# Rotary embedding of the first attention layer: the sine product on VectorE moved behind a pair's score evictions

## The chip, the cores and the metric

The kernel runs on one core of one Trainium2 chip. The metric is device time in microseconds (us) of one execution; lower is better. Before the change it is 1165.88 us, the median of three runs (1165.79 to 1166.37).

## The reference, cut to what matters

Two transformer blocks of two layers each run on a sequence of 256 tokens with model width 1024, in float32. The change touches only the first layer of the first block, whose attention starts like this:

```
z = h @ a_w_in[i]
q = z[..., :w].reshape(B, S, N_DIFF_HEADS, 2, HEAD_DIM)
k = z[..., w:2 * w].reshape(B, S, N_DIFF_HEADS, 2, HEAD_DIM)
...
q = _apply_rope(q, cos, sin)      # [x1*c - x2*s, x2*c + x1*s] over the two halves of each head
k = _apply_rope(k, cos, sin)
...
o_self = _diff_attention(q, k, v, lam, lam_init, a_subln[i])
o_mem = _memory_attention(qm, mem, a_mem_norm[i], a_w_mem_kv[i])
```

So each query and key value is multiplied by a cosine, its partner from the other half of the head by a sine (with a sign), and the two products are added. Only then can the scores of these heads be computed.

## The kernel before, in words

Each engine has its own program, written out in order; engines wait for one another by semaphores. All values are kept transposed: features on the 128 partitions, the 256 tokens along the row. Weights are streamed from HBM in units of 128x1024 into a ring of four slots (`raw`); ScalarE (ACT) rounds a unit to `w_hi` (L1185) and VectorE (DVE) computes the rest `w_lo` (L1651, called a split below). TensorE (PE) multiplies with both.

The stage `in_a` makes query and key tiles of the first layer and runs the attention between them. The function `fused` gives every engine the same frame: step `s` is tile `2s`, then `between(s - 1)`, then tile `2s + 1`, then `behind(s - 1)`. On VectorE these are:

- a tile: `evict` (L1670, PSUM bank times the norm's scale into `Z`, counted by `tile_out`), then the split of a weight unit three tiles ahead;
- `between(p)`: `rotated(j)` for `j = s - 2`, then `normalised` for the two score units of pair `p - 1` (L1979 to L1990: the softmax weights, counted by `p_ready`), then small pieces of later attention steps (L2015, L2022);
- `behind(p)`: `masked` for the two units of pair `p` (L1967: the scores leave their banks, called score evictions here), then L2039 in later steps.

Pair `j` of the six rotary pairs is the query and key tile `2 + 2j` and `3 + 2j` of `Z`. Its rotation has three parts. SyncE (SP), whose program issues weight loads and these transfers in one queue, waits until tile `3 + 2j` has been evicted and then issues four DMAs of 64 KB that exchange the halves of each head into `ROT` (L520, counted by `rot_in`). GpSimd (POOL) multiplies `Z` by the cosine (L2224) at the same time. VectorE multiplies `ROT` by the sine (L2030) as soon as `rot_in` is complete, and adds the two (L2034, counted by `roped`). In the text below, these two are the sine product and the sum.

On TensorE a step is the 24 matmuls of tile `2s`, the output products of an earlier pair, the 24 matmuls of tile `2s + 1`, the scores of pair `p` (L959), and the transposes of the softmax weights of pair `p - 1` (L976), which wait for `p_ready`. TensorE takes all of it in this order. Tiles use two PSUM banks in turn, so tile `t + 2` starts only when tile `t` has been evicted.

The second layer (`in_b`) uses the same functions with another lag; its order stays as it is.

Of the kernel before, what the change touches and what calls it, by code (L numbers as in the profile page):

```python
# [98 lines left out]
FUSED = {"in_a": ("mem_a", "diff"), "in_b": ("mem_b", "moba"), "in_sb": ("stick",), "in_fox": ("forget",)}  # L99
LAG = {"in_a": 1, "in_b": 0, "in_sb": 1, "in_fox": 1}  # L100
# [24 lines left out]
def build_program(nc, ins, out):  # L125
# [7 lines left out]
    with ctx:  # L133
        def sb(name, shape, dt=f32):
            return ctx.enter_context(nc.sbuf_tensor(name, shape, dt))
# [73 lines left out]
        ROT = sb("ROT", [P, 4, TOK])  # L209
# [135 lines left out]
        ROPE_PAIRS = SELF_W // P  # L345
# [82 lines left out]
        def pair_of(name):  # L428

            units = attention_units(name)  # L430

            def pair(p):
                return units[2 * p:2 * p + 2] if 0 <= p < len(units) // 2 else []
            return pair
# [5 lines left out]
        def evicted(name, p):  # L440

            pair, q = pair_of(name), p - AHEAD[name] - 1
            return [pair(at)[1] for at, late in ((q - 1, True), (q, False))
                    if pair(at) and stands_late(name, at) == late]
# [1190 lines left out]
        def _(dve):  # L1635
# [294 lines left out]
            def attention(name):  # L1930
                pair, ahead = pair_of(name), AHEAD[name]
# [7 lines left out]
                def masked(u):  # L1939

                    n, mem = u["n"], u["mem"]
                    _, whole = geometry(u)

                    forget = u["kind"] == "forget"

                    def pieces(ap):
                        return ap.rearrange("p (a c) -> p a c", c=P) if mem or forget else ap

                    def mask(qt, cols):
                        if forget:  # L1950
                            kept = forget_buf[:, n % 4, :].rearrange("p (a c) -> p a c", c=P)
                            return kept[:, 2:3, :] if qt == 0 else kept[:, 0:4:3, :]
                        return no_mask if mem else mask_in[:, cols]
                    b = bank[4 + n % 2]
                    dve.wait_ge(s_done, n + 1)
                    if n >= 4:
                        dve.wait_ge(exp_done, n - 3)
                    if stick:
                        if n - u["first"] >= 4:
                            dve.wait_ge(arg_ready, n - u["first"] - 3)  # L1960
                        nc.vector.scalar_tensor_tensor(s_buf[:, n % 4, 0:whole], b[:, 0:whole], SCALE, mask_ex[:],
                                                       ALU.mult, ALU.add).then_inc(s_out, 1)
                        return
                    if forget:
                        dve.wait_ge(f_ready, n - u["first"] + 1)
                    for qt, cols in enumerate(query_tiles(u)):
                        last = nc.vector.tensor_tensor_reduce(  # L1967
                            out=pieces(s_buf[:, n % 4, cols]), in0=pieces(b[:, cols]),
                            in1=mask(qt, cols), scale=-SCALE, scalar=3.0e38, op0=ALU.add, op1=ALU.min,
                            accum_out=unit_bias[:, n % 4, qt:qt + 1])  # L1970
                    last.then_inc(s_out, 1)
# [50 lines left out]
                    nc.vector.scalar_tensor_tensor(H[:, j, :], H[:, j, :], subln_s[:], sub_rms[:, j % 2, :],  # L2022
                                                   ALU.mult, ALU.mult).then_inc(sub_scaled, 1)

                def rotated(j):

                    pair = ROPE_PAIRS * list(FUSED).index(name) + j
                    rot = ROT[:, 2 * (pair % 2):2 * (pair % 2) + 2, :]
                    dve.wait_ge(rot_in[pair % 2], 64 * (pair // 2 + 1))
                    nc.vector.tensor_tensor(rot, rot, rope_s[:].unsqueeze(1).broadcast_to([P, 2, TOK]),  # L2030
                                            ALU.mult).then_inc(sin_done, 1)
                    dve.wait_ge(sin_done, pair + 1)
                    dve.wait_ge(cos_done, pair + 1)
                    nc.vector.tensor_tensor(Z[:, 2 + 2 * j:4 + 2 * j, :], turned, rot, ALU.add).then_inc(roped, 1)  # L2034

                def sub_low(u):
                    j = u["j"]
                    dve.wait_ge(sub_hi, j + 1)
                    nc.vector.tensor_tensor(o_lo[:, j, :], H[:, j, :], o_hi[:, j, :].bitcast(f32),  # L2039
                                            ALU.subtract).then_inc(sub_lo, 1)  # L2040

                def between(p):

                    j = p + LAG[name] - 2
                    last_tile = 2 * (p + LAG[name]) + 1 == LAST_TILE.get(name)
                    turns = "mem_" in FUSED[name][0] and 0 <= j < ROPE_PAIRS
                    if turns and not last_tile:
                        rotated(j)
                    if stick and p == len(heads["stick"]) // 2 - 1:
                        for u in pair(p):  # L2050
                            masked(u)
                    for u in pair(p - 1):
                        log_weights(u) if stick else normalised(u)
                        if turns and last_tile and u["half"] == 0:
                            rotated(j)
                        if last_tile and u["half"] == (not stick):
                            evict(name, LAST_TILE[name])
                    for u in evicted(name, p):
                        if not u["diff"]:
                            out_lo(u)  # L2060
                    for u in evicted(name, p - 1):
                        if u["diff"]:
                            sub_scale(u)

                def behind(p):

                    for u in pair(p):
                        if not stick or p < len(heads["stick"]) // 2 - 1:
                            masked(u)
                    for u in evicted(name, p - 1):  # L2070
                        if u["diff"]:
                            sub_low(u)
                return between, behind

            nc.vector.memset(log_ms[:], 0.0).then_inc(warm_ready, 1)
# [39 lines left out]
            def lambda_difference():  # L2115
# [6 lines left out]
            values("in_a", {1: lambda: memory_lows(0), 3: memory_sums, 4: lambda: memory_lows(KT // 2)})  # L2122
            dve.wait_ge(tile_out, RING)
            fused("in_a", lambda s: query_key_tile("in_a", s), attention("in_a"), 3,
                  {(0, 0): scale_memory, (0, 1): lambda_sums, (1, 1): lambda_difference, (10, 1): lambda: split_early("out_a")})
            out_projection("out_a", "up_a")
            project("up_a", *relu("up_a"))
            project("down_a", before=residual("down_a", [("in_b", h1_hi, h1_lo), ("q_b", h2_hi, h2_lo)]))
            values("in_b")
            fused("in_b", lambda s: query_key_tile("in_b", s), attention("in_b"), 2,  # L2130
                  {(9, 0): lambda: split_early("out_b")})
            out_projection("out_b", "up_b")
# [3 lines left out]
            values("in_sb", {4: lambda: final_rows(range(0, 3)), 5: lambda: final_rows(range(3, 6)),  # L2136
                             6: lambda: final_rows(range(6, KT))})
            fused("in_sb", lambda s: query_key_tile("in_sb", s), attention("in_sb"), 3,
                  {(8, 0): lambda: split(0, RING, plan["out_sb"]["unit"] + RING - 2, KT),
                   (10, 0): lambda: split_early("out_sb"), (11, 0): lambda: split_early("out_sb", RING)})  # L2140
# [274 lines left out]
```

## Time and profile before

| | before |
|---|---|
| median of 3 runs | 1165.88 us (1165.79 to 1166.37) |
| the profiled execution | 1165.88 us, of which 1164.1 us are the span of the trace |
| busy share of the span | PE 99%, PEld 92%, DVE 76%, ACT 65%, POOL 29% |
| granted TensorE clock, mean | 0.999 of full speed |
| chain that ended last, by engine | PE 88%, DVE 5%, ACT 3%, DMA 1% |

The busy time of PE includes time in which a matmul stands in the pipeline waiting, so 99% is an upper bound of its work. The chain is followed back from the last instruction to what released each one; its shares are over the whole span, and single stages look different.

### The profile page before, as it was taken

How to read it: one execution, taken by the hardware profiler on the slowest of the kernel's cores; microseconds unless marked ns; L12 is line 12 of the kernel's file. 1: busy time of each engine (PE TensorE's matmuls, PEld its weight loads, DVE VectorE, ACT ScalarE, POOL GpSimd, SP SyncE). 2: the span in 40 equal slices, each digit the busy share in tenths (PEclk: the TensorE clock that was granted, in tenths of full speed). 3: DMA queues.
4: the chain of work that ended last, by engine and by line, in shares of the span. 5: the costliest groups of instructions: out<-in, count | busy, mean ns of one | idle time of the engine just before them, and what ended most of it. 6: DMA issues, size and time to landing. Idle time of an engine off the chain costs nothing.

```text
span 1164.1 us, 25960 instructions
## 1 busy us (share of the span) xinstructions
PE 1146.7 (99%) x8640; PEld 1068.2 (92%) x8640; DVE 882.5 (76%) x1494; ACT 753.2 (65%) x1373; POOL 337.9 (29%) x313
## 2 busy tenths in 40 slices
PE   8999999999999999999999999999999999999998
PEld 7988999999898999999899889999889988999987
DVE  7888777666579877766759978999566776898954
ACT  7766655455565755545558878888456666888842
POOL 3230355300012245522303305544000320455500
PEclk9999999999999999999999999999999999999999
DMA  8654556655645455665654346655645634565562
GB/s 316 205 147 140 178 194 202 199 189 189 221 160 162 147 194 192 203 224 181 212 186 146 128 164 195 201 198 198 217 145 186 246 132 141 188 203 200 196 217 101
DMA packets 64054, 216.62 MB, mean 186 GB/s; under 512 B 7776, under 2 KB 10992, under 8 KB 63984
## 3 DMA queue, kind: packets, MB, share of 16 engines
q1 hardware_dynamic: 63808, 215.17, 56.0%
q8 instruction: 41, 0.67, 0.2%
q10 hardware_dynamic: 176, 0.54, 0.1%
q14 instruction: 29, 0.24, 0.1%
HBM read 211.47 MB, written 1.06 MB: 183 GB/s over the span
## 4 chain that ended last, share of the span: by engine, by line
PE 88%; DVE 5%; ACT 3%; DMA 1%; issue 1%; POOL 1%; SPq 0%; DVEq 0%; ACTq 0%; POOLq 0%
PE bank L824 11%; PE bank L825 11%; PE bank L826 11%; PE bank L822 9%; PE bank L819 5%; PE bank L691 4%; PE bank L693 4%; PE bank L692 4%; PE bank L742 4%; PE bank L744 4%; PE bank L743 4%; PE bank L959 2%; PE bank L976 2%; DVE w_lo L1651 2%; PE bank L620 2%; PE bank L621 1%
## 5 line engine op out<-in xcount | busy, mean ns | idle before, releaser
L1651 DVE TENSOR_TENSOR w_lo<-raw,w_hi 128x1024 fp32r<-128x1024 f32 x386 | 507.0, 1324 | 70.3 <-ACT w_hi L1185 69.9
L1185 ACT CAST w_hi<-raw 128x1024 fp32r<-128x1024 f32 x386 | 401.9, 1047 | 220.0 <-PE bank L826 54.2
L824 PE MATMUL bank<-h_hi,w_hi 128*128 128x256 f32 x1184 | 327.0, 276 | 0.4 <-DVE h_lo L1733 0.2
L825 PE MATMUL bank<-h_lo,w_hi 128*128 128x256 f32 x1184 | 325.6, 275 | 0.0
L826 PE MATMUL bank<-h_hi,w_lo 128*128 128x256 f32 x1184 | 325.6, 275 | 0.0
L824 PEld LDWEIGHTS bank<-h_hi,w_hi 128*128 128x128 f32 x1184 | 227.3, 192 | 1.7 <-DVE h_lo L1733 1.2
L825 PEld LDWEIGHTS bank<-h_lo,w_hi 128*128 128x128 f32 x1184 | 227.3, 192 | 0.1
L826 PEld LDWEIGHTS bank<-h_hi,w_lo 128*128 128x128 f32 x1184 | 227.3, 192 | 0.0
L822 PE MATMUL bank<-a,w_hi 128*128 128x512 f32 x496 | 163.3, 382 | 0.0
L691 PE MATMUL bank<-h_hi,w_hi 128*128 128x256 f32 x512 | 144.3, 282 | 0.2 <-ACT v_tok L1432 0.2
L692 PE MATMUL bank<-h_lo,w_hi 128*128 128x256 f32 x512 | 140.8, 275 | 0.0
L693 PE MATMUL bank<-h_hi,w_lo 128*128 128x256 f32 x512 | 140.8, 275 | 0.0
L819 PE MATMUL bank<-a,w_lo 128*128 128x256 f32 x512 | 137.0, 273 | 0.0
L2272 POOL TENSOR_TENSOR prod<-H 128x256 f32<-128x256 f32 x64 | 89.2, 1394 | 82.4 <-DVE H L1782 82.4
L2285 POOL TENSOR_TENSOR conv_buf<-conv_buf,H 128x254 f32<-128x254 f32 x88 | 63.4, 721 | 169.5 <-DVE conv_buf L1812 168.0
L822 PEld LDWEIGHTS bank<-a,w_hi 128*128 128x128 f32 x496 | 93.8, 189 | 12.6
L691 PEld LDWEIGHTS bank<-h_hi,w_hi 128*128 128x128 f32 x512 | 98.2, 192 | 3.3 <-issue 3.3
L819 PEld LDWEIGHTS bank<-a,w_lo 128*128 128x128 f32 x512 | 98.2, 192 | 0.8
L692 PEld LDWEIGHTS bank<-h_lo,w_hi 128*128 128x128 f32 x512 | 98.3, 192 | 0.1
L693 PEld LDWEIGHTS bank<-h_hi,w_lo 128*128 128x128 f32 x512 | 98.3, 192 | 0.0
L1771 DVE TENSOR_TENSOR a<-prod,a 128x256 f32 (+1 forms) x108 | 49.6, 459 | 48.4 <-POOL prod L2272 41.8
L2183 POOL TENSOR_TENSOR sumsq<-sumsq,square 128x256 f32<-128x256 f32 x32 | 31.0, 968 | 154.7 <-ACT square L1197 100.4
(234 smaller groups left out, 2060.5 us busy)
## 6 DMA issues: line engine op xcount, KB each, us to landing
raw<-in_w_up_sb SPq DMA_DIRECT2D x44, 512.0 KB, 4.2
raw<-in_w_up_fox SPq DMA_DIRECT2D x44, 512.0 KB, 3.5
raw<-in_w_up_a SPq DMA_DIRECT2D x32, 512.0 KB, 3.5
raw<-in_w_down_a SPq DMA_DIRECT2D x32, 512.0 KB, 4.7
raw<-in_w_up_b SPq DMA_DIRECT2D x32, 512.0 KB, 4.3
raw<-in_w_down_b SPq DMA_DIRECT2D x32, 512.0 KB, 4.9
raw<-in_w_in_sb SPq DMA_DIRECT2D x24, 512.0 KB, 3.6
raw<-in_w_in_fox SPq DMA_DIRECT2D x24, 512.0 KB, 4.2
```

The lines of the kernel that those rows point to most:

```text
L691: nc.tensor.matmul(dst, w_hi[:, slot, w], in_turns(src_hi[:, k, :]), start=k == 0, stop=False)
L692: nc.tensor.matmul(dst, w_hi[:, slot, w], in_turns(src_lo[:, k, :]), start=False, stop=False)
L693: last = nc.tensor.matmul(dst, w_lo[:, slot, w], in_turns(src_hi[:, k, :]), start=False, stop=k == KT - 1)
L819: last = nc.tensor.matmul(dst, w_lo[:, slot, w], in_turns(src_hi[:, at + k, :]), start=False, stop=False)
L822: last = nc.tensor.matmul(both, w_hi[:, slot, w], pair, start=False, stop=end)
L824: nc.tensor.matmul(dst, w_hi[:, slot, w], in_turns(src_hi[:, at + k, :]), start=begin, stop=False)
L825: nc.tensor.matmul(dst, w_hi[:, slot, w], in_turns(src_lo[:, at + k, :]), start=False, stop=False)
L826: last = nc.tensor.matmul(dst, w_lo[:, slot, w], in_turns(src_hi[:, at + k, :]), start=False, stop=end)
L1185: nc.scalar.copy(w_hi[:, slot, 0:k * P], raw[:, slot, 0:k * P]).then_inc(hi_ready, 1)
L1651: nc.vector.tensor_tensor(w_lo[:, slot, 0:k * P], raw[:, slot, 0:k * P], w_hi[:, slot, 0:k * P].bitcast(f32), ALU.subtract).then_inc(lo_re ...
L2272: nc.gpsimd.tensor_tensor(prod[:, b % 2, :], u_buf[:, b, :], u_buf[:, b, :], ALU.mult).then_inc(prod_ready, 1)
L2285: nc.gpsimd.tensor_tensor(c, c, m_buf[:, b % 2, 0:TOK - 2], ALU.add).then_inc(taps_done, 1)
```

## The change

The sine product gets a function of its own, `sine(j)`. In the stage `in_a` it is issued at the end of `behind`, after the score evictions of the step before; `rotated` then only adds. In the second layer `rotated` still calls `sine` first, so nothing moves there.

```diff
+                def sine(j):
 
                     pair = ROPE_PAIRS * list(FUSED).index(name) + j
                     rot = ROT[:, 2 * (pair % 2):2 * (pair % 2) + 2, :]
                     dve.wait_ge(rot_in[pair % 2], 64 * (pair // 2 + 1))
                     nc.vector.tensor_tensor(rot, rot, rope_s[:].unsqueeze(1).broadcast_to([P, 2, TOK]),
                                             ALU.mult).then_inc(sin_done, 1)
+
+                def rotated(j):
+
+                    pair = ROPE_PAIRS * list(FUSED).index(name) + j
+                    rot = ROT[:, 2 * (pair % 2):2 * (pair % 2) + 2, :]
+                    if name != "in_a":
+                        sine(j)
                     dve.wait_ge(sin_done, pair + 1)
                     dve.wait_ge(cos_done, pair + 1)
                     nc.vector.tensor_tensor(Z[:, 2 + 2 * j:4 + 2 * j, :], turned, rot, ALU.add).then_inc(roped, 1)
...
                         if u["diff"]:
                             sub_low(u)
+                    if name == "in_a" and 0 <= p + LAG[name] - 1 < ROPE_PAIRS:
+                        sine(p + LAG[name] - 1)
```

On VectorE, the rows of the second rotary pair (j = 1) show the pattern of the first five pairs. The ISA rows are the end of the score evictions, L1670 and L1651 are the eviction and the split of the next even tile, and L2034 (L2041 in the changed kernel) is the sum.

```order
 L1967 ISA s_buf,unit_bias<-bank,mask_in_sb 128x256
 L1967 ISA unit_bias 128x1
-L1670 TENSOR_TENSOR Z<-bank,rstd 128x256
-L1651 TENSOR_TENSOR w_lo<-raw,w_hi 128x1024
-L2030 TENSOR_TENSOR ROT<-ROT,rope_s_sb 128x512
-L2034 TENSOR_TENSOR Z<-H,ROT 128x512
+L2030 TENSOR_TENSOR ROT<-ROT,rope_s_sb 128x512
+L1670 TENSOR_TENSOR Z<-bank,rstd 128x256
+L1651 TENSOR_TENSOR w_lo<-raw,w_hi 128x1024
+L2041 TENSOR_TENSOR Z<-H,ROT 128x512
 L1979 RECIPROCAL unit_rcp<-unit_sum 128x2
 L1990 TENSOR_SCALAR p_buf<-p_buf,unit_rcp 128x256 x2
```

The sine product now stands ahead of an eviction and a split and the sum behind them, where both stood behind them before.

For the last pair (j = 5), also on VectorE, the tile that follows belongs to the second layer's memory keys (`ZM`), and the piece L2039 (L2046 in the changed kernel) ends the score evictions.

```order
-L2039 TENSOR_TENSOR o_lo<-H,o_hi 128x256
+L2046 TENSOR_TENSOR o_lo<-H,o_hi 128x256
+L2030 TENSOR_TENSOR ROT<-ROT,rope_s_sb 128x512
 L1670 TENSOR_TENSOR ZM<-bank,rstd_mem 128x256
 L1651 TENSOR_TENSOR w_lo<-raw,w_hi 128x1024
-L2030 TENSOR_TENSOR ROT<-ROT,rope_s_sb 128x512
-L2034 TENSOR_TENSOR Z<-H,ROT 128x512
+L2041 TENSOR_TENSOR Z<-H,ROT 128x512
```

Here too the sine product moves ahead of one eviction and one split. The orders of TensorE, ScalarE, GpSimd and SyncE are unchanged.

## Rows read from the trace of the kernel before

**Rows 1.** The page's first part: busy time, share of the span, instructions
```profile
PE 1146.7 (99%) x8640; PEld 1068.2 (92%) x8640; DVE 882.5 (76%) x1494; ACT 753.2 (65%) x1373; POOL 337.9 (29%) x313
```
**Rows 2.** Windows over six steps, 49.14 to 99.19: sum and mean of busy time
```profile
sum 50.05, PE 48.66 PEld 42.86 DVE 45.83 ACT 31.56 POOL 13.36; mean PE 8.11 PEld 7.14 DVE 7.64 ACT 5.26 POOL 2.23
```
**Rows 3.** The tile ROT, 45 to 110: issues' durations (ns min/median/max), landings
```profile
L520 SPq DMA_DIRECT2D ROT<-Z x24: 512/591/1497, 49.6 to 93.2; - x24
...
DMA to landing us min/median/max: 2.0/2.0/3.1
```
**Rows 4.** Timeline of VectorE, pair j = 1: start, us, instruction, idle before it
```profile
57.70 0.42 DVE L1670 TENSOR_TENSOR Z<-bank,rstd 128x256 f32<-128x256 f32 x1
...
60.54 0.09 DVE L1967 DVE_READ_ACCUMULATOR2_ANT unit_bias<- 128x1 f32 x1
61.21 0.42 DVE L1670 TENSOR_TENSOR Z<-bank,rstd 128x256 f32<-128x256 f32 x1 [0.59 <-PE bank L693]
61.55 1.22 DVE L1651 TENSOR_TENSOR w_lo<-raw,w_hi 128x1024 fp32r<-128x1024 f32 x1
62.68 0.68 DVE L2030 TENSOR_TENSOR ROT<-ROT,rope_s_sb 128x512 f32<-128x512 f32 x1
63.40 0.69 DVE L2034 TENSOR_TENSOR Z<-H,ROT 128x512 f32<-128x512 f32 x1
64.01 0.16 DVE L1979 RECIPROCAL unit_rcp<-unit_sum 128x2 f32<-128x2 f32 x1
...
65.79 0.42 DVE L1670 TENSOR_TENSOR Z<-bank,rstd 128x256 f32<-128x256 f32 x1
```
**Rows 5.** Timeline of SyncE's queue: the four issues of pairs 0 to 3
```profile
49.59 3.29 SPq L520 DMA_DIRECT2D ROT<-Z  x4
...
58.14 2.42 SPq L520 DMA_DIRECT2D ROT<-Z  x4
...
66.23 2.90 SPq L520 DMA_DIRECT2D ROT<-Z  x4
...
75.02 2.41 SPq L520 DMA_DIRECT2D ROT<-Z  x4
```
**Rows 6.** Line L520, pair 0's last two issues: durations (ns), first and last start
```profile
L520 SPq DMA_DIRECT2D ROT<-Z x2: 592/984/1377, 50.9 to 52.3; - x2
```
**Rows 7.** Timeline of VectorE: the sums of pairs 0, 2 and 3
```profile
55.64 0.69 DVE L2034 TENSOR_TENSOR Z<-H,ROT 128x512 f32<-128x512 f32 x1
...
71.85 0.69 DVE L2034 TENSOR_TENSOR Z<-H,ROT 128x512 f32<-128x512 f32 x1
...
79.84 0.69 DVE L2034 TENSOR_TENSOR Z<-H,ROT 128x512 f32<-128x512 f32 x1
```
**Rows 8.** The chain that ended last, pairs 4 and 5: start, us, what
```profile
82.67 0.51 SPq L520
...
85.40 2.02 DMA ROT<-Z
...
87.44 0.71 DVE ROT L2030
...
88.17 0.69 DVE Z L2034
...
91.40 0.51 SPq L520
...
93.22 2.43 DMA ROT<-Z
...
96.40 0.69 DVE Z L2034
```
**Rows 9.** Waits in 49.14 to 99.19: us in total, times, longest
```profile
PEld bank L976 <- DVE p_buf L1987: 2.6, 4, 0.9
PEld bank L976 <- DVE p_buf L1990: 1.4, 3, 0.7
```
**Rows 10.** Windows, 5 to 10: length, busy PE PEld DVE ACT POOL, clock, DMA
```profile
5.00:10.00 5.00, 2.77 (x18) 2.19 (x16) 3.75 (x8) 3.64 (x10) 0.00 (x0) 1.00 0.98 365
```

More of the change, by code:

```diff
@@ L2023, in sub_scale @@
                                                    ALU.mult, ALU.mult).then_inc(sub_scaled, 1)
-                def rotated(j):
+                def sine(j):
                     pair = ROPE_PAIRS * list(FUSED).index(name) + j
```

## The prediction

> **What bounds the kernel now.** The page comes first: TensorE is busy for 99% of the span [rows 1], so over the whole kernel only what makes TensorE wait can cost or give time. But busy time includes matmuls that stand in the pipeline, so the stage itself has to be asked. The change touches six steps, which begin with the odd evictions (L1670) at 49.14, 57.70, 65.79, 74.58, 82.23 and 90.95 and end at 99.19. By the windows over them, TensorE is busy at most 8.11 us of a step that lasts 50.05 / 6 = 8.34 us on average [rows 2]. So it is nearly full, but not quite, and the waits say where the rest goes: to the transposes (L976), which wait for VectorE's softmax weights, 2.6 + 1.4 us in this stretch, up to 0.9 us at a time [rows 9]. VectorE in turn gets there only behind the rotation. The chain that ended last shows this most clearly for pairs 4 and 5: it does not pass through TensorE at all, but runs from an eviction over SyncE's four issues, the landing of ROT, the sine product, the sum and the softmax weights to the next eviction [rows 8]. So there is a loop: odd eviction, issue, landing, rotation, softmax weights, next odd eviction. In the earlier pairs TensorE and this loop are about equally long.
>
> **When the rotated halves are there.** This decides the case, since the sine product now stops everything behind it on VectorE until `rot_in` is complete. After the odd eviction of pair 1 starts (57.70 [rows 4]), SyncE begins its issues at 58.14 and needs 2.42 us for the four [rows 5]; one is 0.59 long [rows 3], so the last starts at 58.14 + 2.42 - 0.59 = 59.97, and a transfer lands 2.0 us after its issue begins [rows 3]: 61.97. The new place of the sine product is behind the score evictions, whose last row is at 60.54 [rows 4]. So it would find its data not there, and VectorE would stand still for about 1.4 us. In the old order the same time is filled: the even eviction starts at 61.21, after 0.59 us of waiting for TensorE, and the split at 61.55, which lets go of the sine product at 62.68 [rows 4]. Only there do the halves already lie in ROT.
>
> The landings of the six pairs, worked out in the same way:
> - pair 0: the last issue starts at 52.29 (49.59 + 3.29 - 0.59; its row says 52.3), landing 54.29 [rows 3, 5, 6];
> - pair 1: 61.97;
> - pair 2: 66.23 + 2.90 - 0.59 + 2.0 = 70.54 [rows 3, 5];
> - pair 3: 75.02 + 2.41 - 0.59 + 2.0 = 78.84 [rows 3, 5];
> - pair 4: 85.40 + 2.02 = 87.42, and pair 5: 93.22 + 2.43 = 95.65, both read from the chain [rows 8].
>
> A rule of the Trainium skill bears on this landing (page "DMA: Bandwidth & Descriptors", section "Anatomy of one DMA"): a DMA costs some 2.0 us whatever its size, plus its bytes at 436 GB/s, mostly because completion must be confirmed; it is fitted to DMAs issued by GpSimd. By it a transfer of 64 KB would be an estimated 2.15 us, so the sum below would be 6 x 0.15 = 0.9 us larger. The trace's median of 2.0 is the measured one for SyncE's queue and is what I use; rule and row alike speak against a landing that is early enough for the new place.
>
> **The change, part by part.** Nothing is added or removed: six sine products, evictions, splits and sums stay as long as they are. What changes is what lies under the wait for ROT. From landing to sum, the new order has: about 0.02 to start the sine product (landing 87.42, start 87.44 [rows 8]); 0.61 until the next instruction can start (the sum, of the same shape, starts at 63.40 and the next row at 64.01); 0.34 for the eviction (61.21 to 61.55); 1.13 for the split (61.55 to 62.68) [rows 4]. Together 2.10 us. The old order has 0.74 there at the least (0.02, and 0.72 from the sine product to its sum, 62.68 to 63.40), or nothing but the end of the split, if that is later. The sums of before start at 55.64, 63.40, 71.85, 79.84 [rows 4, 7], 88.17 and 96.40 [rows 8]. Counted from the same odd eviction, those of after start at landing + 2.10:
> - pair 0: 56.39, which is 0.75 later;
> - pair 1: 64.07, 0.67 later;
> - pair 2: 72.64, 0.79 later;
> - pair 3: 80.94, 1.10 later;
> - pair 4: 89.52, 1.35 later;
> - pair 5: 97.75, 1.35 later.
>
> The sum of these is 6.0 us. Each delay comes on top of the one before, because behind the sum on VectorE stand the softmax weights and the next odd eviction, and that eviction starts the next pair's four issues. The stall does not become cover for anything else: the split and the even eviction that filled it now stand behind it.
>
> Does TensorE already take longer than the new step? In pair 1 the step would be 8.09 + 0.67 = 8.76 us (8.09 is 57.70 to 65.79 [rows 4]), on average 8.34 + 1.0 = 9.3 us, against the at most 8.11 of work [rows 2]. So the loop over VectorE and the transfers now sets every step, and TensorE waits for the rest in front of the transposes. The waits of VectorE for TensorE ahead of the even eviction (0.59 in pair 1 [rows 4]) go away; they are inside the stall, and the differences above already count them.
>
> What else is queued behind the wait? The even eviction starts later (pair 1: 61.97 + 0.02 + 0.61 = 62.60 instead of 61.21, or 1.4 us), and TensorE needs its bank back only two tiles on; the split feeds a unit three tiles ahead, and SyncE's weight load behind it has as much room. I take nothing for these three: two tiles are a step of 8 us, against a delay of 1.4 us. GpSimd's cosine product starts from the odd eviction as before and is not waited for. Past pair 5 no step rotates, and the stages that follow hang on this one, so I let the whole delay reach the end.
>
> **Bounds of the unknown.** SyncE's issues vary between 0.51 and 1.50 us [rows 3]: three of the six pairs have a long one, and which pairs these will be is open. If no pair had one, the last issue would start 1.83 us after the first, as in pair 1: pair 0 would land 0.87 earlier (52.29 - 49.59 - 1.83), pair 2 0.48 (70.54 against 66.23 + 1.83 + 2.0), pair 4 0.9 (85.40 - 82.67 - 1.83), and pair 5, with a landing of 2.0 for 2.43, 0.43; 2.7 in all, and the sum would be 3.3. If all were like pair 4 (2.73 from the first issue to the last, 82.67 to 85.40 [rows 8]), pairs 1, 3 and 5 would lose 0.9 each and pair 2 0.42: 3.1 more, or 9.1. I take the pattern of before, 6.0, as the nearest.
>
> The profiled execution took 1165.88 us, 1.78 beyond its span of 1164.1, and is also the median of the runs. 1165.88 + 6.0 = 1171.9 us. A difference under 0.2%, 2.3 us, is what I count as no change.
>
> **The rivals.**
> - *The sine product fills the wait for TensorE, and the kernel gets faster.* VectorE does wait for TensorE ahead of the even eviction (0.59 us in pair 1), and the sine product has a length of 0.68 [rows 4]. If the halves lay in ROT when the score evictions end, the sum would come 0.72 earlier in each pair, and the transposes' waits (4.0 us [rows 9]) would shrink by up to that: 1165.9 - 4.0 = 1161.9 us at the best. It decides by the landing: the sum comes earlier only if landing + 2.10 is before the old sum, so pair 1 would need its landing 0.67 earlier and pairs 4 and 5 1.35 earlier. No landing is under 2.0 us [rows 3], and the issues cannot start sooner. 4 in 100.
> - *The delay is hidden.* If something else ended the steps (TensorE's own work, say), the 0.67 to 1.35 us would vanish: 1166 us. For it speaks that TensorE is nearly full in the steps; against it, that the transposes already wait, and that the chain of pairs 4 and 5 is the loop itself [rows 8, 9]. 7 in 100.
> - *Half of it is hidden.* Pairs 0 to 2, where TensorE and the loop are about equal, cost nothing, and only pairs 3 to 5 count: 1.10 + 1.35 + 1.35 = 3.8, or 1169.7 us. 14 in 100.
> - *The clock of TensorE falls in the new waits.* They would be some 1.2 us of a step (9.3 - 8.1). At the lower of the two levels, 1.2 GHz, the 8.1 us of a step would take twice as long, so each such step costs up to 8 us: one of them gives 1180 us. The Trainium skill (page "TensorE: Matmul & The Clock Gate", section "HAM oscillation") warns that waits between bursts of matmuls can throttle the engine again. The trace bears it out little: in the stretch from 5 to 10, with only 2.77 of 5.00 us busy, the granted clock is 1.00 [rows 10]. 3 in 100.
>
> **How the numbers follow.** The forecast, all six delays in full, has the remaining 72 in 100; its own bounds are 1169.2 to 1175.0. A range of 1168.8 to 1174.8 also takes in the half-hidden case and leaves out the first two rivals, the clock and the outermost of the long issues, together under 2 in 10. Slower by over 0.2%: forecast, half hidden and clock, 89 in 100. Within 0.2%: 7. Faster: 4.
>
> **What would show it.** In the profile after, VectorE should stand idle ahead of L2030 until DMA ROT<-Z in all six pairs of the first layer (1.4 us in pair 1), and no longer wait for TensorE ahead of the even evictions. The chain that ended last should run through SyncE's issues and the landing in all six steps, which should last from 8.75 us (pair 3: 7.65 + 1.10) to 10.07 us (pair 4: 8.72 + 1.35); the stretch from the first of these odd evictions to the end of the sixth step should be 56 instead of 50 us, and the second layer should look as before. Wrong would be: no idle time there (the landing was earlier than worked out), or idle time with steps as long as before (something else sets them).

## The result, and the profile after

| | before | after |
|---|---|---|
| median of 6 runs | 1166.0 us (1165.74 to 1166.64) | 1171.35 us (1170.57 to 1172.32) |
| the profiled execution | 1165.88 us, span 1164.1 | 1171.27 us, span 1169.5 |
| the six steps of the rotation | 50.05 us [rows 2] | 55.64 us |

The kernel is slower: ratio 1.0046, with a 95% interval of 1.0036 to 1.0056, or 5.35 us between the medians.

The windows over the same six steps of the changed kernel come first (columns as in [rows 2] and [rows 10]; each window goes from one odd eviction to the next).

```profile
48.76:58.24 9.48, 8.23 (x68) 7.12 (x68) 8.38 (x22) 5.51 (x12) 2.12 (x1) 1.00 0.50 160
58.24:66.97 8.73, 8.66 (x74) 7.49 (x74) 7.31 (x22) 5.50 (x13) 2.19 (x1) 1.00 0.50 165
66.97:76.54 9.57, 8.15 (x71) 6.98 (x70) 7.35 (x24) 5.19 (x13) 2.20 (x1) 1.00 0.47 151
76.54:85.27 8.73, 7.66 (x65) 6.87 (x64) 7.01 (x23) 5.66 (x15) 2.19 (x1) 1.00 0.44 142
85.27:95.04 9.77, 8.11 (x67) 7.33 (x68) 7.40 (x23) 3.82 (x12) 2.20 (x1) 1.00 0.46 145
95.04:104.40 9.36, 7.87 (x67) 7.09 (x66) 7.74 (x25) 5.76 (x16) 2.45 (x2) 1.00 0.45 142
sum 55.64, PE 48.67 PEld 42.87 DVE 45.19 ACT 31.45 POOL 13.34; mean PE 8.11 PEld 7.14 DVE 7.53 ACT 5.24 POOL 2.22
```

The work is the same: TensorE is busy for 48.67 us instead of 48.66, and its granted clock is 1.00 in every step. The steps are 5.59 us longer in all, which is the whole difference of the two spans (5.4 us) within 0.2. In pair 1, VectorE's timeline shows what has changed against [rows 4].

```profile
58.24 0.42 DVE L1670 TENSOR_TENSOR Z<-bank,rstd 128x256 f32<-128x256 f32 x1
...
61.09 0.08 DVE L1967 DVE_READ_ACCUMULATOR2_ANT unit_bias<- 128x1 f32 x1
62.51 0.69 DVE L2030 TENSOR_TENSOR ROT<-ROT,rope_s_sb 128x512 f32<-128x512 f32 x1 [1.34 <-DMA ROT<-Z]
63.12 0.42 DVE L1670 TENSOR_TENSOR Z<-bank,rstd 128x256 f32<-128x256 f32 x1
63.46 1.21 DVE L1651 TENSOR_TENSOR w_lo<-raw,w_hi 128x1024 fp32r<-128x1024 f32 x1
64.59 0.69 DVE L2041 TENSOR_TENSOR Z<-H,ROT 128x512 f32<-128x512 f32 x1
```

VectorE stands idle ahead of the sine product for 1.34 us, until ROT has landed. The even eviction behind it starts at 63.12, with no idle time ahead of it, and the split only then. From landing to sum it is 64.59 - 62.49 = 2.10 us. The chain that ended last goes through exactly these places, here in pair 1 (start, us, what):

```profile
58.69 0.51 SPq L520
...
60.51 1.98 DMA ROT<-Z
...
63.54 1.13 DVE w_lo L1651
64.67 0.60 DVE Z L2041
```

In [rows 8] the chain went from the landing straight over the sine product to the sum; now the split lies on it. The chain now takes this way in all six steps, from one odd eviction to the next, without TensorE. Before the change it ran in pairs 1 and 2, and in most of pair 3, through TensorE alone (57.84 to 77.50):

```profile
57.84 0.66 PE bank L976 x4
...
77.50 0.13 PE bank L693
```

So the change did not lengthen a chain that was there in these pairs; it made the loop of issues, landing and rotation longer than TensorE's work. The waits in the six steps (us in total, times, longest) answer to [rows 9]:

```profile
DVE ROT L2030 <- DMA ROT<-Z: 9.8, 6, 2.3
PEld bank L976 <- DVE p_buf L1987: 7.3, 4, 1.9
...
PEld bank L976 <- DVE p_buf L1990: 2.3, 3, 1.7
DVE Z L1670 <- PE bank L693: 1.4, 1, 1.4
```

VectorE waits for ROT in all six pairs, 9.8 us. The transposes wait for the softmax weights for 9.6 us, where it was 4.0. VectorE's wait for TensorE ahead of an eviction is left in one place only, the odd eviction with which the stretch begins.

### The profile page after: what moved, and what is told of

It is laid out like the page before. It is cut to its first block, busy times and chain, and to the rows that moved or that the text cites. A ratio compares the mean times of both kernels' runs of the same rounds, so it can differ in the third digit from the quotient of the medians.

```text
span 1169.5 us, 25960 instructions
## 1 busy us (share of the span) xinstructions
PE 1147.8 (98%) x8640; PEld 1069.0 (91%) x8640; DVE 882.6 (75%) x1494; ACT 752.8 (64%) x1373; POOL 334.8 (29%) x313
## 4 chain that ended last, share of the span: by engine, by line
PE 84%; DVE 6%; ACT 3%; DMA 2%; issue 2%; SPq 1%; POOL 1%; DVEq 0%; POOLq 0%; ACTq 0%
PE bank L824 11%; PE bank L826 11%; PE bank L825 11%; PE bank L822 9%; PE bank L819 5%; PE bank L742 4%; PE bank L743 4%; PE bank L744 4%; PE bank L691 4%; PE bank L693 3%; PE bank L692 3%; DVE w_lo L1651 2%; PE bank L620 2%; PE bank L959 2%; PE bank L621 1%
## 5 line engine op out<-in xcount | busy, mean ns | idle before, releaser
L1651 DVE TENSOR_TENSOR w_lo<-raw,w_hi 128x1024 fp32r<-128x1024 f32 x386 | 507.1, 1324 | 70.4 <-ACT w_hi L1185 70.0
```

The source lines that it names most:

```text
L1651: nc.vector.tensor_tensor(w_lo[:, slot, 0:k * P], raw[:, slot, 0:k * P], w_hi[:, slot, 0:k * P].bitcast(f32), ALU.subtract).then_inc(lo_re ...
```

## The experiments

"Before" ran beside every group of kernels, with medians of 1165.8 to 1165.9 us. The theory: each step is a loop of odd eviction, issues, landing, sine product, what stands between it and the sum, and softmax weights; the change uncovers the wait for the landing and puts an eviction and a split behind it.

**Parts of the change.** Early only for pairs 0 to 2, and only for pairs 3 to 5:

```diff
-                    if name != "in_a":
+                    if name != "in_a" or not j < 3:
                         sine(j)
...
+                    if name == "in_a" and 0 <= j < ROPE_PAIRS and j < 3:
+                        sine(j)
```

> The sine product is early for pairs 0 to 2 only. Theory (all six delays count in full): the first three steps of the changed kernel are 0.92 + 0.64 + 0.78 = 2.3 us longer than before, so about 1168.3 us. Rival (in pairs 0 to 2 TensorE and the loop are about equal, so the delay is hidden there): about 1166.0 us.

> The sine product is early for pairs 3 to 5 only. Theory (the delays of the steps add up): the last three steps of the changed kernel are 1.08 + 1.05 + 1.12 = 3.2 us longer than before, so about 1169.2 us; with the run that had pairs 0 to 2 early (2.2 us above before) it makes up the 5.4 us of the whole change. Rival (one long step late in the stage does it, or the delays overlap): under 1168 us or as slow as the whole change.

Measured: 1168.11 us (ratio 1.0018, 1.0009 to 1.0027) and 1169.07 us (1.0028, 1.0016 to 1.0040). These are 2.2 and 3.1 us above the kernel before, together 5.3 us, against 5.35 for the whole change. So the delays add up. Pairs 0 to 2, where TensorE and the loop are about equal, hide nothing: in the profile of the first run their steps are 28.13 us long instead of 25.44.

**The eviction or the split?** The sine product between the even eviction and the split:

```diff
             def query_key_tile(name, s):
...
                     evict(name, s)
+                if name == "in_a" and s % 2 == 0 and 0 <= s // 2 - 2 < ROPE_PAIRS:
+                    early_sine(s // 2 - 2)
```

> The sine product stands behind the even eviction and ahead of the split only. Theory (the wait for ROT is uncovered; each step is the loop odd eviction, issues, landing, sine product, whatever stands between it and the sum, softmax weights): the six waits stay, a little shorter, but only the split's 1.13 us, not 0.34 + 1.13, lie between landing and sum, so 6 x 0.34 = 2.0 us of the 5.35 come back: about 1169.3 us, slower than before by 3.3. Rival (what costs is the late even eviction, which gives TensorE its bank back late): the eviction is no longer late, so about 1166.0 us, as before.

Measured: 1170.71 us (1.0037, 1.0024 to 1.0051), 1.4 more than expected, with runs from 1169.25 to 1171.83. The profile had one late landing in pair 0 (below), so the same kernel was measured once more.

> The kernel with the sine product between the even eviction and the split, run once more. Its profile had a landing of 4.1 us in pair 0, a stretch of TensorE at a granted clock of 0.66 behind it, and 1171.8 us, where its fastest run took 1169.25. Theory: that was one late landing; a profile without it shows steps 0.3 us shorter than those of the changed kernel and about 1169.3 us. Rival (the late even eviction and the split count otherwise than worked out): again 1170.5 us or more with landings of 2.0 us and the clock at 1.00.

Measured: 1170.68 us (1.0043, 1.0029 to 1.0057), profiled at 1170.16. VectorE's timeline of the second profile, pair 1:

```profile
58.71 0.42 DVE L1670 TENSOR_TENSOR Z<-bank,rstd 128x256 f32<-128x256 f32 x1
...
62.23 0.42 DVE L1670 TENSOR_TENSOR Z<-bank,rstd 128x256 f32<-128x256 f32 x1 [0.59 <-PE bank L693]
62.98 0.69 DVE L1677 TENSOR_TENSOR ROT<-ROT,rope_s_sb 128x512 f32<-128x512 f32 x1 [0.33 <-DMA ROT<-Z]
...
67.11 0.41 DVE L1670 TENSOR_TENSOR Z<-bank,rstd 128x256 f32<-128x256 f32 x1
```

The even eviction comes as soon as TensorE lets it, with the same 0.59 us of waiting as in [rows 4], and the step (8.40 us) is still 0.3 longer than before (8.09); it is 0.33 shorter than in the changed kernel (8.73). So the loss is not that TensorE gets its bank back late; the eviction costs the 0.34 us by which it stood between landing and sum. The other pairs agree: pairs 0, 2, 3 and 5 are 0.35, 0.34, 0.32 and 0.42 us shorter than in the changed kernel, and only pair 4 is 0.03 longer. Its exchange landed later, 5.25 us after the odd eviction instead of 4.89 (the chains have the landings):

```profile
87.01 2.99 DMA ROT<-Z
...
87.53 2.63 DMA ROT<-Z
```

The first line is of this run, the second of the changed kernel. VectorE's waits for ROT halve at the same time, from 9.8 to 4.9 us, while the steps get only 1.7 us shorter (53.91 us, of the 2.0 expected): what counts is the way from landing to sum, and not how long VectorE stands still.

The medians do not show as much: the second run is 4.85 us above the kernel before that ran beside it, where the change is 5.35 above. Both runs missed 1169.3 us. In the second profile, part of the gap lies ahead of the changed code, since its first odd eviction starts at 49.58, where it was 48.76 in the changed kernel; by the end of the sixth step 0.9 of the 1.7 us is left. What the other timed runs had in addition is not settled.

**An earlier landing by a second queue.** ScalarE's queue issues two of the four exchanges, in the changed kernel and in the kernel before:

```diff
-                for piece in range(4):
+                for piece in range(2 if name == "in_a" else 4):
...
+                    for piece in (2, 3):
+                        src, dst = 32 * (piece ^ 1), 32 * piece
+                        nc.scalar.dma_start(ROT[dst:dst + 32, at:at + 2, :],
+                                            Z[src:src + 32, 2 + 2 * j:4 + 2 * j, :]).then_inc(rot_in[j % 2], 16)
```

> The sine product is early for all six pairs as in the change, but ScalarE's queue issues two of the four exchanges, so that the last issue starts some 0.6 us after the odd eviction instead of 1.8 to 2.7 and the landing is 1.2 to 2.1 us earlier. Theory: the landing decides; it now lies about at the end of the score evictions, the sine product fills VectorE's wait for TensorE, and the sums come 0.15 to 0.85 us earlier than before the change: 2 to 2.7 us in all, about 1163.5 to 1164 us, faster than before. Rival (the order on VectorE itself is what costs, the landing is a symptom): still about 1171 us; waits of VectorE for ROT gone, steps as long as in the changed kernel.

> The order of before, with the same early landing by two queues. Theory: before, the sum waits for the split and for the landing only in pairs 4 and 5 (0.26 and 0.16 us), so the early landing alone gives about 0.4 us: 1165.6 us. Rival (an early landing is worth as much in either order): as fast as the kernel with the early sine product and two queues.

Measured: 1168.22 us (1.0022, 1.0013 to 1.0032) and 1166.95 us (1.0008, 0.9999 to 1.0017). Both expectations missed, and the old order is the faster one here, so the second one's rival, equal times, fails too. The chain of the first (early sine product, two queues; pairs 4 and 5) says why:

```profile
83.41 3.64 DMA ROT<-Z
...
92.48 0.52 ACTq L1554
...
93.91 0.48 ACT log_ms L1527
```

Issuing faster did not make the data land correspondingly faster: the exchanges took up to 3.64 us from issue to landing instead of 2.0, and in the kernel with the old order up to 5.3. In pair 5 ScalarE's own issues lie on the chain, since the work behind them is late. The first one's six steps do sum to only 50.92 us instead of 55.64, but the trial changed the landing less than meant and added a cost, so it could not decide.

**An earlier landing without help.** One transfer of 256 KB that leaves the halves where they are, so that the rotation computed is not the reference's, in both orders:

```diff
+                if name == "in_a":
+                    sp.dma_start(ROT[:, at:at + 2, :], Z[:, 2 + 2 * j:4 + 2 * j, :]).then_inc(rot_in[pair % 2], 16)
+                    sp.wait_ge(rot_in[pair % 2], rot_need(pair))
+                    return
                 for piece in range(4):
```

> Sine product early as in the change, but the four exchanges are replaced by one transfer of 256 KB that leaves the halves where they are (so the rotation computed is another one), and SyncE waits for its landing before the next weight load. The issue takes 0.6 us instead of 2.4 to 3.5, and no other engine gets work. Theory (the landing decides): it lies 1.2 to 2 us earlier, about at the end of the score evictions; the sine product then fills VectorE's wait for TensorE, and the sums come up to 0.85 us earlier than in the kernel before: 1163.3 to 1164.8 us. Rival (the order on VectorE costs whatever the landing): 3 us or more slower than its twin with the old order.

> The twin: one transfer of 256 KB without exchange and the same wait of SyncE, with the sine product in its old place. Theory: in the old order the sum hangs on the split in pairs 0 to 3, so an earlier landing gives only the 0.26 and 0.16 us that pairs 4 and 5 waited: about 1165.5 us, 1 to 2 us slower than the early sine product. Rival (an early landing is worth as much in either order): equal times.

Measured: 1165.48 us (0.9997, 0.9988 to 1.0006) with the sine product early, 1165.66 us (0.9998, 0.9989 to 1.0007) with it late. The loss is gone: with an earlier landing the order on VectorE costs nothing, and the rival that blames the order itself falls. But the gain of 1 to 2 us over the twin did not come either; equal times are what the twin's rival said. The timeline of VectorE in the kernel with the early sine product shows both signs, in pair 1 and in pair 2:

```profile
58.01 0.42 DVE L1677 TENSOR_TENSOR Z<-bank,rstd 128x256 f32<-128x256 f32 x1
...
60.85 0.69 DVE L2037 TENSOR_TENSOR ROT<-ROT,rope_s_sb 128x512 f32<-128x512 f32 x1
...
65.41 0.42 DVE L1677 TENSOR_TENSOR Z<-bank,rstd 128x256 f32<-128x256 f32 x1
...
69.25 0.69 DVE L2037 TENSOR_TENSOR ROT<-ROT,rope_s_sb 128x512 f32<-128x512 f32 x1 [1.18 <-DMA ROT<-Z]
...
74.16 0.41 DVE L1677 TENSOR_TENSOR Z<-bank,rstd 128x256 f32<-128x256 f32 x1
```

Pair 1 has no wait for ROT, and its step is 7.40 us long instead of 8.09; pair 2 waits 1.18 us, and its step is 8.75 (before 8.79). Pairs 3 and 5 are like pair 1 (7.57 and 7.76, before 7.65 and 8.24), pairs 0 and 4 wait 0.55 and 1.53 us and lose (9.08 and 9.05, before 8.56 and 8.72). The six steps sum to 49.61 us, those of the twin to 49.46. So the landing decides pair by pair, as the rival "faster" said, and half of the landings were late even with a single transfer (below).

**Two queues where ScalarE has room.** For pairs 0 to 3 only, and SyncE waits for the landing before the next weight load:

```diff
+                shared = name == "in_a" and j < 4
+                for piece in range(2 if shared else 4):
...
+                if shared:
+                    sp.wait_ge(rot_in[pair % 2], 64 * (pair // 2 + 1))
```

> A version that computes the whole reference: for pairs 0 to 3 the sine product is early, ScalarE's queue issues two of the four exchanges, and SyncE waits for the landing before it issues the next weight load; pairs 4 and 5 are as before the change. Theory: without the weight load beside them the exchanges land 2.0 us after the last issue, 3.0 us after the odd eviction starts, and the sums of pairs 1 to 3 come 0.1 to 0.7 us earlier than before: about 1164.5 us, if ScalarE's 1.1 us of issues per pair cost nothing. Rival (ScalarE's issues delay its copies for TensorE, as they did in pair 5 of the first run with two queues): 1166 to 1167 us although the landings are early.

Measured: 1166.38 us (1.0004, 0.9995 to 1.0013). The steps sum to 49.82 us, so nothing is won; VectorE still waits for ROT in each of the four pairs, 0.45 to 1.40 us. The expected 1164.5 us was missed. The time is the rival's (1166 to 1167 us), but not its condition: the landings were not as early as expected, so whether ScalarE's issues cost anything is not shown.

**The split out of the way.** If what lies between landing and sum is the cost, the even split can go elsewhere: behind the next odd eviction, in the kernel before and in the changed one, with the exchanges ahead of that unit's weight load in SyncE's queue:

```diff
+                if name == "in_a" and s % 2 == 0 and 4 <= s < 4 + 2 * ROPE_PAIRS:
+                    return
+                if name == "in_a" and s % 2 == 1 and 5 <= s < 5 + 2 * ROPE_PAIRS:
+                    split(0, RING, g["unit"] + g["values"] + s + RING - 2, KT)
```

> The order of before, but the even tile's split stands behind the next odd eviction instead of ahead of the sine product, and SyncE issues the exchanges ahead of that unit's weight load. Theory (per pair the sum hangs on whichever is later, the landing or the work ahead of it): without the split the sums of pairs 0 to 3 start at landing + 0.74, which is 0.61, 0.69, 0.57 and 0.26 us earlier than before, pairs 4 and 5 as before: about 1163.8 us, faster than both kernels. Rival (TensorE's own work sets the steps of before): about 1166 us.

> The changed kernel (sine product early, all six pairs, four exchanges from SyncE) with the even tile's split moved in the same way, so that only the even eviction's 0.34 us is left between the sine product and the sum. Theory (the cost of the change is what it puts between landing and sum, above all the split's 1.13 us): the sums start at landing + 0.97, 0.38, 0.46, 0.34 and 0.03 us earlier than before in pairs 0 to 3 and 0.23 later in pairs 4 and 5: about 1165 us, so the whole 5.4 us are gone, and some 1.4 us slower than its twin with the sine product late. Rival (VectorE's standing still for ROT is itself the loss, whatever stands behind it): still 3 us or more above before.

Measured: 1166.98 us (1.0008, 0.9999 to 1.0017) and 1167.14 us (1.0012, 1.0003 to 1.0021). Both missed what was expected, 1163.8 and about 1165 us. In the changed order, 1.3 of the 5.35 us are left (1167.14 - 1165.83), and none of them in the six steps, which sum to 49.85 us. Pair 1 there:

```profile
61.87 0.68 DVE L2037 TENSOR_TENSOR ROT<-ROT,rope_s_sb 128x512 f32<-128x512 f32 x1
...
62.80 0.67 DVE L2048 TENSOR_TENSOR Z<-H,ROT 128x512 f32<-128x512 f32 x1
```

The sum starts 0.93 us behind the sine product instead of 2.08. But the splits ahead also cover the landing, so that VectorE waits for ROT for only 0.9 us in all six pairs instead of 9.8. This run alone thus does not tell the wait from what stands behind it; the run with the early eviction does. The exchanges start 0.44 us after the odd eviction, as before the change, so the new order in SyncE's queue did not make the landing earlier.

In both kernels the next step has an extra split: its stretch from the odd to the even eviction is 4.05 us instead of 3.00. The rest of what the medians have above the steps is not settled.

The gain with the old order failed: its steps sum to 49.53 us, only 0.5 less than before, and the next step takes more than that back. In its timeline, VectorE's two splits and GpSimd's cosine product stand as follows:

```profile
56.90 3.44 DVE L1654 TENSOR_TENSOR w_lo<-raw,w_hi 128x1024 fp32r<-128x1024 f32 x2
...
57.06 2.19 POOL L2231 TENSOR_TENSOR H<-Z,rope_c_sb 128x512 f32<-128x512 f32 x1 [5.53 <-DVE Z L1673]
```

Two splits should take 1.13 + 1.22 = 2.35 us; they took 3.44. The second would have started at 58.03, inside the product of 57.06 to 59.25, and ended 1.09 us behind that product. So the score evictions, and with them the sine product, came late (5.41 us after the odd eviction instead of 4.98), and so did the sum.

**Both splits out of the way, the second one after GpSimd's product.**

```diff
+                    odd = 2 * (p + LAG[name]) + 1
+                    if name == "in_a" and 5 <= odd < 5 + 2 * ROPE_PAIRS:
+                        g = plan[name]
+                        split(0, RING, g["unit"] + g["values"] + odd + RING - 1, KT)
                 return between, behind
```

> The order of before with both splits moved out of the way of the sum and of GpSimd's cosine product: the even tile's split stands directly behind the next odd eviction, the odd tile's split behind the score evictions, and the exchanges go ahead of the even unit's weight load. In the run with both splits behind the odd eviction the second one took 2.3 us instead of 1.2, since it started while GpSimd's product ran, and the score evictions and the sine product came later than the landing. Theory: the second split now starts after that product has ended (some 2.9 us after the odd eviction) and lies under the wait for ROT; the sums of pairs 0 to 3 start at landing + 0.74, 0.26 to 0.69 us earlier than before: about 1163.8 to 1164.5 us, faster than both kernels. Rival (the steps of before are set by TensorE's own work and ScalarE's chain, so an earlier sum gives nothing): 1165.8 us or more, with TensorE no longer waiting for the softmax weights.

Measured: 1164.91 us (0.9995, 0.9986 to 1.0004), with the profiled run at 1164.45; expected were 1163.8 to 1164.5. VectorE's timeline, pair 1:

```profile
57.15 0.42 DVE L1673 TENSOR_TENSOR Z<-bank,rstd 128x256 f32<-128x256 f32 x1
57.49 1.22 DVE L1654 TENSOR_TENSOR w_lo<-raw,w_hi 128x1024 fp32r<-128x1024 f32 x1
...
59.99 1.22 DVE L1654 TENSOR_TENSOR w_lo<-raw,w_hi 128x1024 fp32r<-128x1024 f32 x1
61.13 0.42 DVE L1673 TENSOR_TENSOR Z<-bank,rstd 128x256 f32<-128x256 f32 x1
61.49 0.69 DVE L2038 TENSOR_TENSOR ROT<-ROT,rope_s_sb 128x512 f32<-128x512 f32 x1
62.22 0.69 DVE L2042 TENSOR_TENSOR Z<-H,ROT 128x512 f32<-128x512 f32 x1
...
64.60 0.42 DVE L1673 TENSOR_TENSOR Z<-bank,rstd 128x256 f32<-128x256 f32 x1
```

The splits fill the time until the landing, both at 1.22 us, and the sum follows the sine product directly. The step is 7.45 us long, and the six sum to 47.75 us, 2.3 less than before and 7.9 less than in the changed kernel. TensorE is busy for 47.61 us of them, so the windows show next to no wait of it there. Of the 2.3 us, 1.4 us reach the span of the profiled run and 1.0 the median; the next step, which has an extra split, gives 1.0 back (its odd-to-even stretch is 4.04 us instead of 3.00). It is clearly faster than the changed kernel; against the kernel before, the interval still holds 1, so a gain there is not shown.

## Why the prediction was right

The forecast was 1171.9 us, the measured median 1171.35, and the mechanism is the one forecast: the loop over VectorE and the transfers sets all six steps, with 8.73 to 9.77 us each. The steps of the prediction, one by one:

- **The halves are not there at the new place.** Right: VectorE waited in all six pairs, in pair 1 for 1.34 us (worked out: 1.4). The landings took 2.02, 1.98, 2.00, 1.98, 2.63 and 2.21 us from the last issue, so in pairs 0 to 3 the measured 2.0 fits and not the estimate of 2.15; with the two late ones the mean is 2.14.
- **2.10 us from landing to sum.** Right to the hundredth in pair 1.
- **The six delays.** Worked out: 0.75, 0.67, 0.79, 1.10, 1.35, 1.35, together 6.0 us. Measured as differences of the steps: 0.92, 0.64, 0.78, 1.08, 1.05, 1.12, together 5.59. The terms of pairs 4 and 5 were too large by 0.3 and 0.2: I carried over the long issue of pair 4 (2.73 us from first issue to last) and the late landing of pair 5 (2.43). In the changed kernel pair 4's last issue came 1.82 us after its first, though its landing was later (2.63), and pair 5 landed after 2.21. Pair 0's term was too small by 0.17, as its four issues took 3.46 us instead of 3.29. That pairs 0 to 3 otherwise kept the issues of before was taken over and not explained, so the closeness of the sum is in part luck.
- **TensorE's room.** The 8.11 us that the prediction took as the most that TensorE is busy in a step are the mean of six unequal steps. In pairs 1 to 3 it was busy nearly throughout:

```profile
57.70:65.79 8.09, 8.02 (x69) 6.91 (x68) 7.40 (x22) 5.09 (x13) 2.20 (x1) 1.00 0.60 178
65.79:74.58 8.79, 8.77 (x76) 7.54 (x75) 7.44 (x24) 5.62 (x14) 2.20 (x1) 1.00 0.53 152
74.58:82.23 7.65, 7.65 (x65) 6.87 (x64) 7.09 (x23) 5.09 (x15) 2.19 (x1) 1.00 0.53 157
```

  So the rival that hides the delay behind TensorE's work was nearer than the mean made it look. The delays of these pairs came in full all the same (0.64, 0.78 and 1.08 us).
- **The delays add up and reach the end.** Right: 2.2 + 3.1 = 5.3 us for the two halves apart, and 5.59 us in the steps become 5.4 in the span; what follows the six steps takes 1065.1 us instead of 1064.9.
- **The even eviction, the split's unit and the weight load cost nothing by being late.** The run with the early eviction bears this out for the eviction: it gave back 0.33 us in pair 1, the 0.34 that it takes, and no more. The other two were not tried alone.
- **The rival "faster".** Its condition was named rightly: pair 1 with one transfer had no wait and a step 0.7 us shorter. Over all pairs it gave no gain, since every second landing stayed late.
- **The hidden cases** fell with the run of pairs 0 to 2 alone.
- **The clock** did not fall in the changed kernel. That it can is shown by another run (below), so this rival was of the right kind, and its condition did not come.

## What to carry to other kernels

Before an instruction is moved ahead in an in-order queue to fill a wait, work out when its data lands, from the last of the issues and not the first: here the gap was real, but the data came 1.0 to 2.3 us later, and the work that used to cover that time moved behind it. The better move was the other one: leave the waiting instruction last, and bring work that nobody waits for into the time ahead of it (1164.91 us, against 1171.35; over the kernel before, a gain is not shown). A place that looks free on one engine can still collide with another (here a split with GpSimd's product), so look at what else runs there.

## What the runs showed of the hardware

- **A split of VectorE and GpSimd's product wait for each other.** In the run with both splits behind the odd eviction and the old order, a split that started inside the product took 2.3 us instead of 1.22 and ended 1.09 us after it. The Trainium skill (page "SBUF — State Buffer", section "SBUF: two separate sides") says that the two engines share a pair of ports, held exclusively for a whole instruction by whichever starts first; the trace agrees, with the 2.3 us. A split that started 0.16 us ahead of the product kept its 1.22 us in the last run (57.49 against 57.65). The product then pays: its usual 2.20 us include such a split, since the one in the kernel before that met none at its start (the sixth of the second layer) took 1.27 us. In pair 5 of the run with both splits both splits went ahead of it at full speed, and it took 3.33 us:

```profile
90.83 2.35 DVE L1654 TENSOR_TENSOR w_lo<-raw,w_hi 128x1024 fp32r<-128x1024 f32 x2
...
90.99 3.33 POOL L2231 TENSOR_TENSOR H<-Z,rope_c_sb 128x512 f32<-128x512 f32 x1 [6.44 <-DVE Z L1673]
```

- **Instruction transfers coincide with long issues and late landings.** With one transfer per pair and the old order, the stretches of the exchange show this in pairs 2 and 3 (queue, kind: packets, MB, share; then the issue with its us to landing):

```profile
q8 instruction: 1, 0.02, 1.6%
ROT<-Z SPq DMA_DIRECT2D x1, 256.0 KB, 3.5
...
ROT<-Z SPq DMA_DIRECT2D x1, 256.0 KB, 2.3
```

In pairs 0, 2 and 4 one packet of instructions moves on queue q8 in that time, and the landing takes 4.3, 3.5 and 3.6 us; in pairs 1, 3 and 5 there is none, and it takes 2.3 each time. In the kernel before and in the changed one, too, the pairs 0, 2 and 4 are those with such a packet, and the long issues are all among them, as is the landing of 2.63 us. Pair 5, whose landings took 2.43 and 2.21 us, has a packet on another instruction queue, q14. It is a coincidence in three traces; no run took the packets away.
- **TensorE's clock can fall in such waits.** In the first run with the eviction ahead, the exchange of pair 0 landed 4.13 us after its last issue. The windows there (length, busy PE first, the granted clock third from the end):

```profile
56.00:58.00 2.00, 0.77 (x8) 0.34 (x4) 2.00 (x4) 0.84 (x1) 0.00 (x0) 1.00 0.01 2
58.00:60.00 2.00, 1.08 (x9) 0.85 (x9) 1.93 (x9) 0.46 (x1) 0.07 (x1) 1.00 0.72 236
60.00:62.00 2.00, 2.00 (x13) 2.00 (x11) 2.00 (x8) 1.01 (x3) 2.00 (x1) 0.54 0.33 91
```

TensorE was busy for 1.85 of 4.00 us, and then its granted clock was 0.54, so nearly all of that stretch ran at the lower of its two levels, 1.2 GHz. Its matmuls then started 0.21 us apart instead of 0.11, until 63.6, and the step of pair 1 took 9.60 us, against 8.40 in the second profile of the same kernel. In the changed kernel's profile every step has 1.00. Of the ten runs with the early sine product and two queues for all pairs, the three slowest (1169.98 to 1170.64 us) have a mean granted clock of 0.997 or 0.998, the others 0.999 or more.
